# A decoder layer on one core: attention of all chunks ahead of the state-space work of chunks 2 and 3, with ring rows, PSUM banks and weight loads rearranged

## What is computed

```
h = h + hybrid_mixer(rms_norm(h))   # attention | ssd_scan, joined, @ w_out
h = h + peer(rms_norm(h))
out = rms_norm(h, norm_final)

def peer(xn, ...):                   # per token, 8 heads
    q = xn @ w_query                 # two halves per head
    s1, s2 = q0 @ sub_keys1.T, q1 @ sub_keys2.T
    v1, i1 = top_k(s1, 16); v2, i2 = top_k(s2, 16)
    top_s, pos = top_k(v1[:, None] + v2[None, :], 16)
    idx = i1 * 128 + i2 at pos;  gates = softmax(top_s)
    pre = einsum(expert_down[idx], xn);  act = gelu(pre) * gates
    return einsum(act, expert_up[idx])
```

## Time and profile before

| | |
|---|---|
| median of 3 runs | 1539.23 us (1537.77 to 1543.08) |
| the profiled execution: its own time | 1540.8 us |
| its span | 1539.0 us |
| busy: PE, DVE, POOL, ACT | 86%, 70%, 43%, 25% |
| gathers (the software queue q0) | 73,728 packets, 536.90 MB |
| all bytes read | 566.23 MB |

### The profile page before, as it was taken

How to read it: one execution, slowest core, us unless ns; L and a number is a source line. 1 busy time by engine, 2 the same in 40 slices (tenths; PEclk the granted TensorE clock), 3 DMA queues, 4 the chain that set the end, 5 groups by cost and what they waited for, 6 DMA issues and landing times.

```text
span 1539.0 us, 13720 instructions
## 1 busy us (share of the span) xinstructions
PE 1326.4 (86%) x4368; PEld 689.2 (45%) x4368; DVE 1072.2 (70%) x2665; ACT 379.4 (25%) x1007; POOL 660.8 (43%) x541
## 2 busy tenths in 40 slices
PE   8999989997778888888888988888888888789877
PEld 4556874443334444444444444444443434444433
DVE  3546898786777767677776776778677776767754
ACT  2114262121212222222222222222222222222221
POOL 0001135543455545445455444554544544554441
PEclk9999999999999999999999999999999999989998
DMA  7740069999999999999999999999999999999995
GB/s 254 195 166 1 28 255 408 408 421 417 419 421 415 422 421 409 421 413 411 421 421 406 412 421 408 422 415 412 399 422 421 418 422 401 423 416 414 408 421 225
DMA packets 88044, 570.80 MB, mean 371 GB/s; under 512 B 10115, under 2 KB 15524, under 8 KB 21540
## 3 DMA queue, kind: packets, MB, share of 16 engines
q0 software_dynamic: 73728, 536.90, 84.8%
q1 hardware_dynamic: 14244, 33.03, 6.4%
HBM read 566.23 MB, written 3.67 MB: 370 GB/s over the span
## 4 chain that ended last, share of the span: by engine, by line
DMA 51%; PE 33%; DVE 10%; ACT 3%; issue 2%; POOL 1%; SPq 0%; DVEq 0%; ACTq 0%; POOLq 0%
DMA arena<-in_experts_du_dram,arena 50%; PE ps L1374 21%; PE ps L1142 5%; DVE arena L965 5%; PE ps L1313 2%; ACT arena L571 1%; PE ps L1348 1%; DVE arena L977 1%; ACT arena L560 1%; POOL wide L389 1%; PE ps L1129 1%; PE ps L1165 0%; DVE arena L862 0%; PE ps L1157 0%; ACT arena L435 0%
## 5 line engine op out<-in xcount | busy, mean ns | idle before, releaser
L1374 PE MATMUL ps<-arena 128*128 128x512 f32 x1588 | 764.1, 629 | 119.7 <-ACT arena L571 119.5
L389 POOL DMA_INDIRECT arena<-in_experts_du_dram,arena x409 | 515.7, 1261 | 484.3 <-PE ps L1374 409.4
L1374 PEld LDWEIGHTS ps<-arena 128*128 128x128 f32 x1588 | 315.6, 203 | 535.5 <-issue 378.9
L965 DVE CUSTOM_DVE_ANT_0 arena<-arena,wide 128x1024 f32<-128x1024 f32 x204 | 246.8, 1224 | 120.9 <-DMA arena<-in_experts_du_dram,arena 120.0
L965 DVE CUSTOM_DVE_ANT_0 arena<-arena 128x1024 f32<-128x1024 f32 x205 | 248.1, 1225 | 112.4 <-DMA arena<-in_experts_du_dram,arena 111.4
L1374 PE MATMUL ps<-wide,arena 128*128 128x512 f32 x412 | 213.6, 644 | 71.3 <-ACT arena L571 71.0
L560 ACT ACTIVATE arena<-arena 128x4 f32<-128x4 f32 (+2 forms) x133 | 27.3, 205 | 929.6 <-DVE arena L965 929.6
L389 POOL DMA_INDIRECT wide<-in_experts_du_dram,arena x103 | 127.5, 1238 | 206.6 <-PE ps L1374 184.3
L571 ACT ACTIVATE arena<-ident,arena 128x128 f32<-128x128 f32 x500 | 160.6, 390 | 47.6 <-DVE arena L977 47.6
L1374 PEld LDWEIGHTS ps<-wide,arena 128*128 128x128 f32 x412 | 77.7, 199 | 172.7 <-ACT arena L571 94.4
L1142 PE MATMUL ps<-arena 128*128 128x512 f32 x192 | 83.2, 593 | 0.0
(11 more groups left out here) (181 smaller groups left out, 987.8 us busy)
## 6 DMA issues: line engine op xcount, KB each, us to landing
arena<-in_w_in_blocks_dram SPq DMA_DIRECT2D x16, 512.0 KB, 10.3
arena<-in_experts_du_dram,arena POOLq DMA_INDIRECT x409, 13.7
wide<-in_w_query_dram SPq DMA_DIRECT2D x5, 1024.0 KB, 9.8
wide<-in_w_out_dram SPq DMA_DIRECT2D x1, 4096.0 KB, 17.8
h<-in_x_dram SPq DMA_DIRECT2D x4, 512.0 KB, 9.2
arena<-in_w_query_dram SPq DMA_DIRECT2D x2, 1024.0 KB, 7.1
wide<-in_experts_du_dram,arena POOLq DMA_INDIRECT x103, 13.2
arena<-in_x_t_dram SPq DMA_DIRECT2D x3, 512.0 KB, 6.4
```

Of the source, the lines that this page charges most:

```text
L389: gp.indirect_dma_start(rows[b], None, experts_du, bass.IndirectOffsetOnAxis(ap=idx[:, (q // PH) % 2, q % PH * TOPK + i:q % PH * TOPK + i ...
L965: v.tensor_tensor_reduce(down, down, xn2[s // SLOTS % 2], 1.0, 0.0, ALU.mult, ALU.add, pre[:, s % 16:s % 16 + 1]).then_inc(sem("dots"), 1)
L1374: last = mm(acc(t, b)[:], diag(s), up[:, b * 512:(b + 1) * 512], start=(s % SLOTS == 0), stop=False, skip_group_check=True)
```

## The change

It rearranges the hand-written lists. On every engine the attention of chunks 2 and 3 moves ahead of the state-space steps of these chunks, and much of it ahead of `query(0)`. The state-space steps of chunks 2 and 3 come after the first `routed`. The time steps and decays (`time_steps`, `decay_sums`, `to_chunk_end`) are made in one go after the second q block. On GpSimd the gathers get another order (0, 1, 5, 3, 2, 4, 6, 10, 7, 8, 9, 11, 13, 12, 14, ...) and other waits; the ten row buffers, the z buffers of chunks 2 and 3, two weight buffers and the diagonals' buffer change places, and tile 0 accumulates in PSUM banks 6 and 7 in place of 4 and 5. `mixT_sb` is split into `mixA_sb` and `mixS_sb`. SyncE issues the weights of head 3 only after `gated` reached 4 (all four gates; before, behind `z_ps`), one half of head 4's weights behind them, and the other half after `wo_half` reached 4.

```
-        zs = [slot(19)[:, 0:512], slot(19)[:, 512:], slot(22)[:, 512:], slot(23)[:, 512:]]
+        zs = [slot(19)[:, 0:512], slot(19)[:, 512:], slot(0)[:, 0:512], slot(0)[:, 512:]]
-                  ((0, wide), (2, wide), (0, arena), (2, arena), (6, wide), (8, wide), (10, wide))]
+                  ((0, wide), (2, wide), (2, arena), (0, arena), (6, wide), (8, wide), (10, wide))]
-        rows = [slot(14, 2, wide), slot(4, 2), slot(6, 2), slot(9, 2), slot(12, 2, wide), slot(0, 2, arena2),
-                slot(2, 2, arena2), slot(20, 2), slot(22, 2), slot(11, 2)]
+        rows = [slot(14, 2, wide), slot(4, 2), slot(6, 2), slot(0, 2, arena2), slot(2, 2, arena2), slot(20, 2),
+                slot(22, 2), slot(12, 2, wide), slot(9, 2), slot(11, 2)]
-        MIX_BANKS = [(0, 1), (3, 3), (3, 3), (3, 3)]
+        MIX_BANKS = [(0, 1), (6, 0), (6, 3), (3, 3)]
-            return ps[4 + 2 * (t % 2) + b]
+            return ps[6 - 2 * (t % 2) + b]
...
             for q in (2, 3):
+                if q == 3:
+                    sp.wait_ge(sem("gated"), NT)
                 sp.dma_start(w_head[q], ...
-            sp.wait_ge(sem("wo_half"), 4)
-            sp.wait_ge(sem("row_free"), PE_DONE[TOPK - 1])
-            for j in range(2):
+            sp.wait_ge(sem("off_ps"), NT - 1)
+            for j in (1, 0):
+                if j == 0:
+                    sp.wait_ge(sem("wo_half"), 4)
                 sp.dma_start(w_head[4][:, :, j, :], ...
...
                 elif s == 3:
+                    gp.wait_ge(sem("score_sb"), 4 * NT)
+                elif s == 5:
+                    gp.wait_ge(sem("score_ps"), 2 * NT)
+                elif s in (4, 6):
+                    gp.wait_ge(sem("pv_ps"), NT)
+                elif s == 7:
+                    gp.wait_ge(sem("mixS_ready"), NT)
+                elif s == 8:
                     gp.wait_ge(sem("y_ps"), NT)
                     gp.wait_ge(sem("off_read"), NT - 1)
-                elif s == 4:
-                    gp.wait_ge(sem("mixS_ready"), NT)
-                elif s == 5:
-                    gp.wait_ge(sem("score_sb"), 4 * NT)
-                elif s == 6:
-                    gp.wait_ge(sem("pv_ps"), NT)
...
             def mixed(c, part):
                 act.wait_ge(sem(("mixA_ps", "mixS_ps")[part]), c + 1)
+                if part == 0 and c > 1:
+                    act.wait_ge(sem("off_ps"), c - 1)
```

More of the change, by code:

```diff
@@ L417, in _ @@
             gather(11)
+            gather(13)
             gather(12)
-            gather(13)
             gather(14)
@@ L1028, in _ @@
+            z_product(2)
             search_sums(0)
             search_indices(0)
-            attended(1)
+            scores(3, 0)
+            ssd_masks(2)
+            z_product(3)
+            scores(3, 1)
+            maxima(3)
+            ssd_state(2)
+            dots(0, 1)
+            dots(1, 1)
             ssd_diagonal(2)
-            ssd_norm(1)
-            scores(2, 0)
-            z_product(2)
+            ssd_segments(3)
+            ssd_norm(2)
             ssd_inputs(3)
-            scores(2, 1)
@@ L1037, in _ @@
-            maxima(2)
-            ssd_segments(3)
-            dots(0, 1)
-            ssd_norm(2)
-            search_halves(1)
-            attended(2)
-            gates(0, 1)
-            dots(1, 1)
-            scores(3, 0)
             ssd_masks(3)
             ssd_state(3)
-            scores(3, 1)
-            maxima(3)
+            gates(0, 1)
+            attended(3)
+            gates(1, 1)
             ssd_diagonal(3)
-            z_product(3)
-            search_sums(1)
+            dots(2, 2)
@@ L1467, in _ @@
-            turn_probs(2, 3)
+            query(0)
+            turn_probs(2, 2)
+            keyed(0)
+            turn_probs(2, 3)
+            attend(2)
+            ssd_off(2)
+            turn_mix(2, 0)
+            scores(3, 0)
+            project_z(3)
+            scores(3, 1)
+            query(1)
+            ssd_state(2)
+            turn_mix(1, 1)
+            ssd_diagonal(2)
+            ssd_segments(3)
+            turn_probs(3, 0)
+            ssd_start(3)
+            turn_probs(3, 1)
@@ L1486, in _ @@
+            turn_mix(3, 0)
+            experts(0, 1)
+            turn_mix(2, 1)
+            experts(1, 1)
             turn_mix(3, 1)
-            experts(1, 1)
-            turn_mix(3, 0)
+            query(2)
+            pieces(8, 12)
+            pieces(0, 4)
             experts(2, 2)
-            pieces(2, 4)
+            experts(4, 4)
+            experts(8, 4)
             pieces(4, 8)
             keyed(2)
-            experts(4, 4)
-            pieces(8, 12)
-            experts(8, 4)
+            experts(12, 4)
```

267 lines of the change are left out of this document (125 added, 142 removed).

## The result

The changed kernel takes **1546.39 us** in the median of 16 runs (1539.51 to 1551.19), the kernel before 1539.51 in the median of 16 (1536.12 to 1543.08): a ratio of **1.0045, interval [1.0032, 1.0057]**, or 6.9 us more. The prediction was 1542.7 with a range from 1536 to 1549, and "within 0.3%" was its likeliest outcome; the time lies in the range, but 3.7 above the forecast and on the slower side of the bound. The profiled execution took 1547.22.

A forecast was written before the change was run, and what follows sets the result against it. The stream of gathers, gapless from 241 us on full DMA engines, was taken as the bound: 1540.8 + 0.8 (ramp) + 2.7 (wait at query(4)) = 1544.3, less 1.6 for the median gives 1542.7 us, range 1536 to 1549.

The forecast's parts named there:

- within 0.3%: Whole kernel: time within 4.6 us of the kernel before, between 1534.6 and 1543.8; chance 0.53.
- slower (0.34): Whole kernel: time above the 1543.8 border; chance 0.34.
- the rival with the longer VectorE list: Ramp: seven meetings with GpSimd steps lengthen VectorE's list to the last norm by 5.1 us; 1547 with the stand; chance 0.13.
- The first gather: about 14 us later.: Front, chunk 0 to first gather: TensorE's sum puts query(0) at 176.0 and the first gather at 193, before 179.
- The ramp: nearly all of it is given back: First gather to 241 us: mixS_ready at 224.8, stream only 0.35 MB or 0.8 us behind.
- a reserve of 2: VectorE's list from routed to mixS_ready: 2 us allowed for waits on TensorE and GpSimd, beside 30.8 of work.
- The weights of head 4: Second half for query(4): issued at 267 at the earliest, 23.4 us to landing, landed at 290.5.
- The price of the stand: TensorE waits about 5 us at query(4) for weights; four gathers in a thin queue cost 2.7 us, bounds 0 and 5.0.
- Thin: Gathers behind the wait at query(4): queue does not stop but moves 331 GB/s for 421, 0.68 us for each gather.
- The bound in which the whole stand goes through: Wait at query(4): upper bound on its price, 5.0 us, all of TensorE's wait lost by the stream.

The follow-up runs named there:

- e2: Changed kernel with gather(8) moved on GpSimd ahead of gate(3); 1547.33 us, ratio 1.0056 to the kernel before.
- e12: Changed kernel with GpSimd's add_off and gate steps of chunks 2 and 3 cut to one column in place of 512; 1547.54 us, ratio 1.006.
- e4: Kernel before with query(4) alone moved up on TensorE directly behind query(3); 1551.58 us, ratio 1.0082.
- e1: Changed kernel with query(4) moved back on TensorE behind the experts of slots 36 to 39; 1543.11 us, ratio 1.0025.
- e9: Changed kernel with query(4) behind pieces(20, 24) and pieces(32, 36) behind the experts of slots 40 to 43 on TensorE; 1541.21 us, ratio 1.0018.

## Why the prediction was nearly right, and where it failed

**The place of the losses** was right: ramp and `query(4)`, nothing behind them. **The chances.** The time is in the range, but the likeliest outcome, within 0.3% (0.53), did not come; slower (0.34) did, by 0.45%. The nearest single figure, the 1547 of the rival with the longer VectorE list, has a ramp loss of 5.1 and the same 2.7 for the stand; the stream showed 4.4 and 6.5, so that it came near is luck in part.

**"The first gather: about 14 us later."** 193 forecast, 193.47 measured where the clock stayed up (e2), with `query(0)` at 176.11 for 176.0: the sum over TensorE's steps was right. What is missing is the clock: on the mean of nine executions the gather went out at 196.8. I had counted each step of chunk 0 at the full clock.

**"The ramp: nearly all of it is given back"**, 0.8 us. This step failed; it measured 3.2 at 241 us and 4.4 at 297. `mixS_ready` came at 231.7 and not at 224.8: 3.1 from the front, the rest in VectorE's list. That list took 36.6 us from `routed` for 32.8 forecast: 30.4 without the meetings and the wait (30.8 forecast, right), 4.95 for the meetings with GpSimd and 1.26 for a wait on TensorE, against a reserve of 2. The late front is not needed for the loss: e2's first gather went out as forecast, its last norm ended at 230.2, and its stream was 4.3 us behind before at 297. The long list was the rival given 0.13, with "seven, 5.1 us". Its mechanism is real, and the rule of the Trainium skill (SBUF — State Buffer, "SBUF: two separate sides") held for all five meetings, each with a VectorE step of two SBUF inputs, but for the 0.5 us by which the first outlasts `state_decay`. Its price at the end did not show: e12 took half of it away, moved the stream by 1.2 us at 297 and gained no time, under the stand. What a shorter list gives without the stand no run tests, so this part of the ramp's loss is argued and not shown.

**The weights of head 4.** 24.9 us to landing, where 23.4 was worked out from the earlier trace rows: right. The issue came at 274.0, not at 267, since `wo_half` 4 hangs on the late ramp; hence 298.9 and not 290.5. TensorE came at 289.6 for 284.8, so the stand was 9.4 and not 5.

**The price of the stand** was 2.7 us, with bounds of 0 and 5. Measured 6.5 in the stream, for a stand nearly twice as long: a term of the right kind and too small by 3.8. "Thin" was the wrong picture: between 297 and 315 the engines were busy for 0.71, and a stand of 14.2 brought that to 0.36. The bound in which the whole stand goes through was the better price, less up to 3 us. The lower clock behind it (5.84 for 3.73) is part of that.

**What did not add up.** 0.8 + 2.7 was forecast and 10.9 is what the stream shows at 330, but the time is only 6.9 longer. 4.4 us come back in this pair of profiles because that one execution of before moved less between 400 and 1200 than any other. Typical executions of before must then have been later at 400 than this one. e4 shows 1.3 us of that at 270; the rest stays open, as does what exactly makes the clock fall in chunk 0. So the range held partly by luck: both terms were too small by 7.4 us in the stream, and with all 10.9 in the time it would have been some 1550, outside the range of 1536 to 1549.

**The two losses are not independent.** The landing of the weights fixed the stream's place at 330 us whatever the ramp had done, and the stand covered the hole of 4 us that e1 laid bare. With stand and hole mended (e9) 1.0018 is left. By the stream it was lost ahead of 297; that it is the later front and the longer VectorE list is the likeliest reading, but no experiment took either away alone. None of the twelve beats the kernel before.

## What to carry to other kernels

When a stream feeds a ring of buffers, look for the longest stretch in which the engine that frees buffers does something else, be it a wait or work. What it has over the depth of the queue is lost whole, and the largest such hole hides the smaller ones ahead of it and behind it, so mend it first and look again. A load of small pieces that must run beside a full stream wants its own lead, here 25 us for half a megabyte where 6 do while few gathers are queued. An order that is right for one engine is right only with the lists of the others: put back alone, the old order of chunk 0 cost 5 us. And a loss ahead of such a hole cannot be priced by its time before the hole is gone; read it in the bytes moved up to there.

## What the runs showed of the hardware

- TensorE's clock may fall to the lower level in one execution and not in the next, with the same instructions: 1.00 to 0.50 over 126 to 135, behind a z product and two idle times of 0.6 us, and 6.5 us between the earliest and the latest first gather. The order of before stayed at 1.00 with idle times of 0.98 and 0.59 in the same part of chunk 0, so these alone do not tell what brings the clock down. It may be part of the wider spread of the changed kernel (11.7 us over 16 runs, against 7.0); no run shows that.
- VectorE steps of one column wait for a GpSimd step of 512: 1.01 and 1.22 for 0.16 and 0.22. A gather issued by GpSimd did not lengthen the dot product beside it (1.22, at 207.80 beside the issue at 207.06), but the first mask step stood from 196.61 on, 0.6 us ahead of `state_decay`, beside the issue of the first gather. Which of the two holds in general stays open.
- VectorE steps that read PSUM were not lengthened beside a GpSimd step of 512 (L866, 1.42 for two beside `skip(2)`). GpSimd can be the one that waits: `gate(3)`, which began behind the start of a dot product, took 2.30 for 1.28.
